# Shift and scale columns by pairs of contraction tiles, with the first six tiles of the input product accumulated beside them

## The reference, cut to what matters

```python
def modulation(cvec, w_mod, b_mod):
    m = jax.nn.silu(cvec) @ w_mod + b_mod
    return m.reshape(cvec.shape[0], N_MOD, 1, D_MODEL)

def trunk_layer(x, mod, h0, g, w_in, ...):
    hn = rmsnorm(x, g[0]) * (1.0 + mod[:, 1]) + mod[:, 0]
    z = hn @ w_in
    x_lru, y_gate, b_g, c_g, v = jnp.split(z, [...], axis=-1)
    xc = (dwconv(x_lru, cw, (2, 1)) + cb)
    ...  # two scans over xc per head, gated by block-diagonal products of xc
    x = x + mod[:, 2] * (jnp.concatenate([lru_out, sc_out], axis=-1) @ w_out)
    hn = rmsnorm(x, g[1]) * (1.0 + mod[:, 4]) + mod[:, 3]
    f = (jax.nn.silu(hn @ w_gate) * (hn @ w_up)) @ w_down
    return x + mod[:, 5] * f, ...
```

## Time and profile before

| | us |
|---|---|
| median of 3 runs | 1820.32 |
| lowest and highest | 1819.82, 1820.63 |
| the profiled execution | 1819.35 |
| span of its profile | 1817.5 |
| TensorE busy in the span | 1751.0 |
| VectorE, ScalarE, GpSimd busy | 810.2, 603.9, 79.8 |
| moved by DMA | 307.30 MB |

### The profile page before, as it was taken

One profiled execution on the slowest core, in us unless ns is written; L12 is line 12 of the kernel. 1 busy time (PEld: TensorE's weight loads), 2 busy tenths in 40 slices (PEclk: granted clock), 3 DMA queues, 4 the chain that ended last, 5 costly groups with the idle time before them and its releaser, 6 DMA issues.

```text
span 1817.5 us, 24801 instructions
## 1 busy us (share of the span) xinstructions
PE 1751.0 (96%) x10189; PEld 1642.6 (90%) x10189; DVE 810.2 (45%) x1187; ACT 603.9 (33%) x678; POOL 79.8 (4%) x106
## 2 busy tenths in 40 slices
PE   5889999999999989999999999999999999999997
PEld 2359989998889878999999999999999999999996
DVE  1155445644463346344353535344443535353445
ACT  1152444444652235222323232222223232322226
POOL 1210010000100000000000000000000000000000
PEclk8879999999999999999999999999999999999998
DMA  9976566665666664734343333334343434333321
GB/s 369 380 261 232 191 207 229 220 216 197 214 207 219 201 225 145 252 116 139 116 135 119 130 124 125 129 119 134 116 138 115 138 115 135 119 130 124 124 85 70
DMA packets 210587, 307.30 MB, mean 169 GB/s; under 512 B 5228, under 2 KB 152992, under 8 KB 210160
## 3 DMA queue, kind: packets, MB, share of 16 engines
q1 hardware_dynamic: 192272, 239.10, 39.2%
q0 software_dynamic: 18064, 67.53, 10.3%
q10 hardware_dynamic: 208, 0.08, 0.0%
HBM read 303.54 MB, written 3.15 MB: 169 GB/s over the span
## 4 chain that ended last, share of the span: by engine, by line
PE 93%; DMA 4%; DVE 2%; ACT 1%; issue 0%; ACTq 0%; SPq 0%; DVEq 0%
PE psum L1145 29%; PE psum L1147 28%; PE psum L1146 28%; PE psum L1167 4%; DMA raw<-in_w_mod 3%; PE psum L1267 1%; PE psum L1177 1%; DMA raw<-in_w_in 0%; DMA ident<-in_tables 0%; DVE act_lo L789 0%; DVE scratch L774 0%; DVE w_lo L734 0%; PE psum L1236 0%; PE psum L1247 0%; DVE scratch L778 0%
## 5 line engine op out<-in xcount | busy, mean ns | idle before, releaser
L1145 PE MATMUL psum<-act_hi,w_hi 128*128 128x384 f32 x2304 | 779.8, 338 | 17.5 <-DVE act_lo L789 14.9
L734 DVE TENSOR_TENSOR w_lo<-raw,w_hi 128x1024 fp32r<-128x1024 f32 x376 | 458.3, 1224 | 725.6 <-ACT w_hi L459 725.2
L1147 PE MATMUL psum<-act_hi,w_lo 128*128 128x384 f32 x2304 | 771.4, 335 | 0.0
L1146 PE MATMUL psum<-act_lo,w_hi 128*128 128x384 f32 x2304 | 771.2, 335 | 0.0
L459 ACT ACTIVATE w_hi<-raw 128x1024 fp32r<-128x1024 f32 x376 | 395.6, 1059 | 854.1 <-PE psum L1147 808.3
L1145 PEld LDWEIGHTS psum<-act_hi,w_hi 128*128 128x128 f32 x2304 | 433.8, 188 | 34.6 <-issue 28.2
L1146 PEld LDWEIGHTS psum<-act_lo,w_hi 128*128 128x128 f32 x2304 | 433.8, 188 | 2.1
L1147 PEld LDWEIGHTS psum<-act_hi,w_lo 128*128 128x128 f32 x2304 | 433.6, 188 | 0.0
L1145 PE MATMUL psum<-h_hi,w_hi 128*128 128x384 f32 x704 | 235.7, 335 | 0.9 <-DVE h_lo L1038 0.9
L1147 PE MATMUL psum<-h_hi,w_lo 128*128 128x384 f32 x704 | 235.2, 334 | 0.0
L1146 PE MATMUL psum<-h_lo,w_hi 128*128 128x384 f32 x704 | 235.2, 334 | 0.0
(11 more groups left out here) (128 smaller groups left out, 578.8 us busy)
## 6 DMA issues: line engine op xcount, KB each, us to landing
raw<-in_w_mod POOLq DMA_DIRECT2D x62, 1024.0 KB, 7.3
raw<-in_w_gate SPq DMA_DIRECT2D x44, 1024.0 KB, 5.1
raw<-in_w_up SPq DMA_DIRECT2D x44, 1024.0 KB, 5.0
raw<-in_w_down SPq DMA_DIRECT2D x44, 1024.0 KB, 5.0
raw<-in_w_in SPq DMA_DIRECT2D x40, 1024.0 KB, 5.1
raw<-in_w_mod SPq DMA_DIRECT2D x34, 1024.0 KB, 9.1
raw<-in_w_out SPq DMA_DIRECT2D x16, 1024.0 KB, 5.2
stage<-in_x_sample SPq DMA_DIRECT2D x2, 1024.0 KB, 15.9
```

Source lines behind the costliest of these rows:

```text
L734: dve.tensor_tensor(split_view(w_lo, b), source, split_view(w_hi, b).bitcast(F32), ALU.subtract).then_inc(lo_ready, 1)
L1145: pe.matmul(psum[:, bank, 0:T], hi, x_hi, start=first, stop=False)
L1146: pe.matmul(psum[:, bank, 0:T], hi, x_lo, start=False, stop=False)
L1147: return pe.matmul(psum[:, bank, 0:T], lo, x_hi, start=False, stop=last)
```

## The change

The 24 groups of modulation columns stay. The first eight no longer hold 512 neighbouring columns: group `p` now holds the 256 shift columns and the 256 scale columns of the two contraction tiles 2p and 2p+1, so that after group `p` this pair of activations can be made. Beside them TensorE multiplies each finished pair with the first six output tiles of `w_in` (768 columns) and accumulates in six PSUM banks over all eight pairs. The last two x tiles (`N_X3`) follow as four blocks, and then step 2 of the old order.

```diff
+    X_TILES = 6
+    X_LOADS = 5 * (KT // 2)
+    N_X3 = KT
+    N_IN = N_X3 + 4
+        X_BANKS = (2, 3, 0, 1, 4, 5)
...
+            def wait_for_slot(load):
+                pair, part = divmod(load, 5)
+                if part:
+                    sp.wait_ge(mod_used, 4 * pair + part)
+                else:
+                    sp.wait_ge(lo_ready, 2 * pair + 2)
+            def x_step(pair):
+                for part in range(5):
+                    number = 5 * pair + part
+                    slot, _ = x_load(pair, part)
+                    if number >= SLOTS:
+                        wait_for_slot(number - SLOTS)
+                    if part == 0:
+                        sp.dma_start(raw[slot][:, 0:2 * X_WIDE]..., w_in_v[:, 2 * pair:2 * pair + 2, 0:X_WIDE])
                     else:
+                        q = part - 1
+                        for m in range(2):
+                            at = m * D + 256 * pair
+                            sp.dma_start(raw[slot]...[:, :, m, :], w_mod_v[:, 4 * q:4 * q + 4, at:at + 256])
-            m_step(0)
             sp.dma_start(x_rows[:, 0, :], x_prompt[0]).then_inc(x_landed, 16)
...
-            with sp.Fori(1, MOD_FIRST) as i:
-                m_step(i)
-            gm_step(N_IN, w_in_v, PHASES[0][1], MOD_FIRST, first=True)
-            gm_step(N_IN + 8, w_in_v, PHASES[0][1] + 512, MOD_FIRST + 1)
+            for pair in range(KT // 2):
+                x_step(pair)
```

GpSimd loses its eight multiplications. ScalarE and VectorE run by pairs:

```diff
-            pool.wait_ge(rstd_ready, 1)
-            for pair in range(KT // 2):
-                pool.tensor_tensor(mix[:, tiles, :], xT[:, tiles, :], rstd..., ALU.mult)
...
+            for pair in range(KT // 2):                       # ScalarE
+                act.wait_ge(hat_ready, pair + 1)
+                norm_pair(0, 0, pair, mix[:, 2 * pair:2 * pair + 2, :])
+                if pair + 1 < KT // 2:
+                    round_x(2 * pair + 2)
+                    round_x(2 * pair + 3)
...
+            hat_pair(0)                                       # VectorE
+            for pair in range(KT // 2):
+                copy_row(pair)
+                add_pair_bias(pair)
+                dve.wait_ge(hat_ready, pair + 1)
+                scale_ctx(pair)
+                low_act(pair)
+                if pair + 1 < KT // 2:
+                    hat_pair(pair + 1)
+                    subtract_x(2 * pair + 2)
+                    subtract_x(2 * pair + 3)
+                if pair == 1:
+                    decays()
```

In the new names `x_mod_quarter(p, q)` is a quarter of group `p`, `x_product(p, half)` is half of the products of one contraction tile (3 output tiles by 3 matmuls, so four of them are a pair), `hat_pair` is the multiplication by the reciprocal root, `round_x` and `subtract_x` split one contraction tile of `w_in` (768 columns), and `wait_for_slot` is the wait for a raw buffer. TensorE's order:

```diff
-            for m in range(1, 5):
-                mod_step(m, range(0, 1))
-                ... tokens turned, sum_squares(m - 1)
-                mod_step(m, range(1, 4))
...
+            turn_x(1)
+            turn_x(2)
+            sum_squares(1)
+            turn_x(3)
+            x_mod_quarter(0, 0)
+            sum_squares(2)
+            turn_x(4)
+            x_mod_quarter(0, 1)
+            sum_squares(3)
+            x_mod_quarter(0, 2)
+            sum_squares(4)
+            x_mod_quarter(0, 3)
+            turn_row(0)
+            for pair in range(1, KT // 2):
+                x_mod_quarter(pair, 0)
+                x_product(pair - 1, 0)
+                x_mod_quarter(pair, 1)
+                x_product(pair - 1, 1)
+                x_mod_quarter(pair, 2)
+                x_mod_quarter(pair, 3)
+                x_product(pair - 1, 2)
+                turn_row(pair)
+                x_product(pair - 1, 3)
+            for half in range(4):
+                x_product(KT // 2 - 1, half)
...
+            pe.wait_ge(padded_ready, 2)
+            for b in range(4):
+                gemm_block(N_X3 + b, "GM", b, 2, act_hi, act_lo, 4 * b, b == 0, b == 3)
+                if b % 2:
+                    mod_half(MOD_FIRST, b // 2)
```

More of the change, by code:

```diff
@@ L294, in landings, with x_load, x_raw @@
             if kind == "GM":
[L295 to L298, removed]
+                return X_LANDED + 16 * (block // 4 + 1) + 4 * (n - N_X3)
+            earlier = 0 if block // 2 % 2 else 4 * (N_G1 - N_X3)
+            return X_LANDED + earlier + 16 + 2 * (n - N_G1)
+        def x_load(pair, part):
+            load = 5 * pair + part
+            return load % SLOTS, sum(16 if earlier % 5 == 0 else 32 for earlier in range(load % SLOTS, load + 1, SLOTS))
+        X_LANDED = x_load(KT // 2 - 1, 4)[1]
+        def x_raw(k):
+            slot, _ = x_load(k // 2, 0)
+            return raw[slot][:, X_WIDE * (k % 2):X_WIDE * (k % 2) + X_WIDE]
         block_ctx = ctx.enter_context(nc.Block())
@@ L1169, in mod_quarter, with x_mod_quarter, mod_half @@
                 out.then_inc(mod_used, 1)
+            def x_mod_quarter(pair, q):
+                slot, landing = x_load(pair, 1 + q)
+                if pair and q == 0:
+                    pe.wait_ge(row_ready, pair)
+                pe.wait_ge(landed[slot], landing)
+                mod_matmuls(q, slot)
+            def mod_half(m, half):
+                if half == 0:
+                    pe.wait_ge(row_ready, m)
+                for i in range(2):
+                    pe.wait_ge(mod_landed[i], m * 32 + 16 * (half + 1) - 32 * MOD_FIRST)
+                    mod_matmuls(2 * half + i, 2 * i + 1)
             def turn_row(m):
@@ new lines, in turn_x, with x_product @@
+                out.then_inc(x_turned, 1)
+            def x_product(pair, half):
+                k = 2 * pair + half // 2
+                if half == 0:
+                    pe.wait_ge(act_ready, pair + 1)
+                if half % 2 == 0:
+                    pe.wait_ge(lo_ready, k + 1)
+                for tile in range(3 * (half % 2), 3 * (half % 2) + 3):
+                    cols = slice(tile * P, (tile + 1) * P)
+                    out = product(X_BANKS[tile], w_hi[k % SLOTS][:, cols], w_lo[k % SLOTS][:, cols],
+                                  act_hi[:, k, :], act_lo[:, k, :], k == 0, k == KT - 1)
+                    if k == KT - 1 and tile == 1:
+                        out.then_inc(x_pair_done, 1)
+                if half % 2:
+                    out.then_inc(block_done, 1)
```

444 lines of the change are left out of this document (252 added, 192 removed).

## The result

The changed kernel takes **1827.61 us** (median of 14 runs, 1822.26 to 1834.77; a fifteenth, at 6490.25 us with a mean granted clock of 0.263, is left out as disturbed). The kernel before took 1820.32 (15 runs, 1819.49 to 1821.21). The ratio is 1.0041, with a 95% interval of 1.0034 to 1.0048: about 7 us slower. The profiled execution took 1828.08, its span 1826.2, which is 8.7 more than before.

A forecast was written before the change was run, and what follows sets the result against it. Bound: a chain closing through the weights' buffer. Start 41.0, pair 0's period 16.0, six periods 97.2 and 14.9 give 169.1; against 163.2, +5.9 us on 1819.35 is 1825.3, median 1826 us, range 1812 to 1839.

The forecast's parts named there:

- The closed chain: Each pair's fourth quarter waits for the weights' split, which waits for the previous pair's fourth quarter: 15.3 us a period.
- The start: Lead-in up to pair 0's fourth quarter, landing at 41.0 us; DMA stands still for some 16 us.
- the ladder: In the lead-in, TensorE and ScalarE alternate turns, squarings and sums; pair 0's fourth quarter is issued only at 35.8 us.
- The clock: TensorE waits 2.9 us for each landing; half clock then makes periods 16.65 us, in four of six.
- rival 3: Every wait for a fourth quarter leaves the clock slow: +8.6 us, or 1829; chance 0.13.
- Behind the six tiles: Last two x tiles, step c and second norm: losses and gains taken to cancel, 0 us.
- The narrow place at step c: Third block of step c, three convolutions ahead of its split: costs between nothing and 1.5 us.
- E: Time the new kernel has the six x tiles done, put at 169.1 us; against 163.2, +5.9 us.
- tail: From the landing of pair 7's fourth quarter until the six x tiles are done: 14.9 us with slow clock.
- Full clock: Rival: no period slow, all at 15.3 us or less: -2.6 us, or 1817.7; chance 0.2.
- The hidden chain: Rival: shorter landing and links, so DMA sets 14.5 us a period: -7.3, or 1813; chance 0.12, shared with a shorter start.
- The late recovery: Rival: clock returns only behind the row's turn, period 18.2 us: +19.3, or 1840; chance 0.15, shared with a longer start.

The follow-up runs named there:

- e1: Changed kernel with the `w_in` weights in a place of their own and one raw buffer per `w_mod` quarter: 1805.95 us, ratio 0.9924 to the kernel before.
- e2: Changed kernel with nine more products (1.56 us, to a bank nobody reads) ahead of each fourth quarter: 1823.62 us, ratio 1.0008 to the kernel before.
- e5: Kernel of e1 with each `w_mod` quarter loaded as 512 neighbouring columns, 2 KB rows, one DMA: 1799.76 us, ratio 0.9881 to the kernel before.
- e6: Changed kernel with the first tile of weights rounded and split one sum of squares earlier: 1824.82 us, ratio 1.0033 to the kernel before.
- e3: Changed kernel with the multiplication by the reciprocal root back on GpSimd, all eight pairs at once: 1826.21 us, ratio 1.0029 to the kernel before.
- e7: Changed kernel with VectorE splitting the weights first and multiplying by the reciprocal root behind that: 1820.01 us, ratio 0.9997 to the kernel before.

## Why the prediction was right, point by point

**The closed chain: right.** It was put at 15.3 us a period at full clock from ten rows of the kernel before; the one period at full clock took 15.37. In it the splits ended 9.68 us after the quarter's start (said: 10.1) and the next quarter began 5.69 behind them (said: 5.2), so two small errors cancel; the others began 5.1 to 5.4 behind the splits, but for one. e1 shows that it was the bound: without it a pair takes 14.0.

**The start: the ladder was right, 1.8 us short.** The fourth quarter was to be issued at 35.8 and to land at 41.0; it was issued at 37.56 and landed by 42.77. The first turn began at 13.89 in place of 13.1, and the first sum of squares ran at the slow clock, 4.04 us in place of the 2.75 of the earlier trace rows. DMA stood still for 15 us, from about 23 to 38, but for GpSimd's loads near 34; 21 to 36 was said. Pair 0's period was 15.56 where 16.0 was said, in part since its quarter took 1.69 and not 1.94.

**The clock: its price was right, the choice of four in six was not.** Four of six periods were taken as slow; five were, four of them at 16.29 to 16.65 us against the predicted 16.65. The sixth is no wait that left the clock alone: the quarter at 58.33 waited only 0.85 us, since TensorE was late with pair 0's slow products. Each of the six waits of 2.1 us or more, pair 7's included, was followed by a slow stretch. That is what rival 3 says. The waits were mostly 2.1 us and not the 2.9 that were said, and only two quarters took the 1.9 us that was named as the sign, 1.89 at 73.70 and 1.93 at 125.28 (behind a wait of 3.77). In the others the slow stretch began later, latest in the period from 106.52:

```profile
106.52 1.07 PE L1270 MATMUL psum<-raw,cond_w 128*32 128x512 f32 x8 [2.10 <-DMA raw<-in_w_mod]
...
110.24 1.71 PE L1296 MATMUL psum<-select,mod_row 128*128 128x2 f32 x8
...
114.19 0.52 PE L1250 MATMUL psum<-act_lo,w_hi 128*128 128x384 f32 x1
```

That period, of 18.76 us, is the longest. Its splits ended 11.8 us after the quarter's start (11.1 to 11.3 in the other slow ones), and the next quarter began 6.96 behind them, so most of its excess is a late landing. SP's issue of the weights behind that quarter also took long (start us, us; SP's queue):

```profile
102.35 0.51 SPq L364 DMA_DIRECT2D raw<-in_w_in  x1
...
119.32 2.73 SPq L364 DMA_DIRECT2D raw<-in_w_in  x1
```

It stands behind the late quarter and so didn't delay it; both may have one cause, which no run shows. In e2's profiled execution all four late landings stood beside ordinary issues of the weights (0.51 us). The six periods were to take 97.2 and took 99.9; of these 2.7 us, 2.1 are that one period. Rival 3 has 99.9 too, with six slow periods; that it agrees to the tenth is luck, since the measured sum holds a period at full clock and one with a late landing.

**Behind the six tiles: taken as 0, measured -1.2.** The narrow place at step c (0 to 1.5 us) cost nothing: no wait stands there. The second norm gave back 1.3 us (9.9 to 8.6), more than the 0.3 to 0.6 expected. So that term was mis-sized, and the other absent.

**The sum.** E was to be 169.1 and is 173.1: start +1.8, pair 0 -0.4, six periods +2.7, tail 14.9 as said. With -1.2 behind it (the difference that is left, and TensorE's idle time there did shrink by 1.2) the span grows by 173.1 - 163.2 - 1.2 = 8.7. The forecast said 5.9. For the profiled execution it was thus 2.8 us short, for the median 1.6.

**The rivals.** Full clock (1817.7) did not come. Up to the splits a slow period took 1.4 to 1.6 us more than the 9.68, and 2.1 in one, where 1.35 was said; the whole periods differ by only 0.9 to 1.3, but for the longest, because the one at full clock ended in a landing 0.5 us later than most. e2 supports that the clock has a price of its own, with 4.0 us back for more work. The hidden chain (1813) did not come, since the links together were no shorter; with the chain open e1 even goes below it, mainly because my 338 GB/s for 1 KB rows was too low. It is 357 when DMA is full, 14.0 us a pair and not 14.5: I had scaled the 322 by the share of 1.05 from 2 KB rows, and with 1 KB rows a full share is 1.09. With 2 KB rows it is 390, as the earlier trace rows had it, and with the chain open (e5 against e1) this difference is worth 6.2 us. The rule of the page "DMA: Bandwidth & Descriptors" in the Trainium skill (section Specifications), line rate from 512 B on, does not hold here: 357 against 390. The two kernels differ in one thing more, since the 2 KB rows of a quarter come in one DMA and the 1 KB rows in two. All periods slow (1829) was near, for five in six were, and all behind a wait of 2.1 us or more. The late recovery (18.2 us a period) did not come as a rule: behind the slow quarter of 73.70 the clock was back before the turn of the row. In the period from 106.52 it did last through the turn (1.71 us) and the nine products behind it, until about 114.7. As the quarter there was at full clock, it cost up to the splits only 0.6 us more than in the other slow periods. The rule of the page "TensorE: Matmul & The Clock Gate" in the same skill (section "HAM oscillation — how this bites in real kernels"), a start at half clock behind each DMA wait, held for each of the six waits of 2.1 us or more, though not always at the quarter itself. The waits of the page's kernel are 3 to 5 us long, so it says nothing of the 2.9 us to which the prediction applied it, nor of 2.1; and in e6 a wait of 2.37 us was followed by 6 us at the whole clock.

**Where the gain went.** The change does start the products 60 us earlier: the first stands at 50.69 us in place of 111.16. But one of the five loads of a pair goes through a buffer that VectorE frees only behind the activations of the pair before. Per pair that costs 1.4 us over what DMA needs at full clock, and the wait that it makes costs 1 to 1.5 us more in clock in most pairs. The version with the weights in a place of their own keeps the gain: 14 us under the kernel before.

## What to carry to other kernels

Count the loads per round against the buffers: where they are one more, a load can come to wait for the round's last consumer, and the round becomes a chain through every engine plus a full landing, which no engine's share of busy time shows. Break it by giving the odd load its own place (21.7 us here), before making a link shorter (7.6 us). And price TensorE's wait twice, once as time and once as the clock that it leaves behind, because that part also has a share in how far the runs scatter.

## What the runs showed of the hardware

- **GpSimd beside VectorE.** While GpSimd multiplied (eight instructions, 14.90 us, 1.86 each), VectorE's 128x4 instruction took 1.73 us in place of 0.16, two scalings of 128x128 took 3.56 in place of 0.60, and two subtractions of 128x768 took 3.44 in place of 1.82 (e3 against the changed kernel). That fits a wait for up to one of GpSimd's instructions at a time. The page "SBUF — State Buffer" of the Trainium skill (section "Who interferes with whom") says as much: a VectorE instruction with two inputs in that memory, or in a mode that uses both of its port pairs, and a GpSimd instruction that reads it exclude each other for a whole instruction.
- **The clock behind a wait.** Each of the six waits of 2.1 us or more before a fourth quarter, behind about 5 us of dense work, was followed by a stretch at 1.2 GHz. Where it began differed: four waits of 2.10 or 2.11 us left the quarter at 1.89, 1.28, 1.07 and 1.50 us in the same execution, and behind the 1.07 the clock was low a little later and for longest (mean 0.81 in that period). In e7, waits of 1.18 to 1.83 left every quarter at 1.06 or 1.07, and one of 2.25 did not (1.14, period at 0.90). But in e6 a wait of 2.37 was followed by 6 us at the whole clock, so the length of the wait does not decide alone. In the old lead-in, where the work is thinner, waits of 1.27 and 1.38 were enough.
- **Row size.** DMA at full share (1.09 and 1.05) carried 357 GB/s in rows of 1 KB, two DMAs to a quarter, and 390 in rows of 2 KB, one DMA to a quarter (e1 and e5).
- **A landing** of 1 MB: the fourth quarter began 5.1 to 5.7 us behind the splits in six of the seven periods and 6.96 in one, with the same work around it. In e2's profiled execution four of seven came 6.8 to 7.4 behind, in e3's one 9.2. The cause is open. In a closed chain the whole kernel waits for such a one.
